# Scan of a hybrid prefix model on one Trainium2 core: output products with the two heads in turn, score products as two 64-row tiles

## The reference, cut to what matters

```
def step(s, inp):
    r_t, w_t, k_t, v_t, kk_t, a_t = inp
    sa = jnp.einsum("bhvk,bhk->bhv", s, kk_t)
    s = (s * w_t[:, :, None, :] - sa[..., None] * (kk_t * a_t)[:, :, None, :]
         + v_t[..., None] * k_t[:, :, None, :])
    return s, jnp.einsum("bhvk,bhk->bhv", s, r_t)
```

## Time and profile before

| | |
|---|---|
| Median of three runs | 2352.16 us (2350.6 to 2354.79) |
| Span of the profiled execution | 2351.2 us; the page gives no other time for it |
| Busy: PE | 1999.7 us (85%) |
| Busy: PE weight loads | 1426.2 us (61%) |
| Busy: DVE | 1150.0 us (49%) |
| Busy: ACT | 717.7 us (31%) |
| Busy: POOL | 179.3 us (8%) |
| DMA over the span | 291.82 MB, mean 124 GB/s |

### The profile page before, as it was taken

How to read it: one execution, slowest core, us unless ns; L and a number is a source line. 1 busy time by engine, 2 the same in 40 slices (tenths; PEclk the granted TensorE clock), 3 DMA queues, 4 the chain that set the end, 5 groups by cost and what they waited for, 6 DMA issues and landing times. The chain is left out here.

```text
span 2351.2 us, 28632 instructions
## 1 busy us (share of the span) xinstructions
PE 1999.7 (85%) x9873; PEld 1426.2 (61%) x9873; DVE 1150.0 (49%) x1761; ACT 717.7 (31%) x1046; POOL 179.3 (8%) x230
## 2 busy tenths in 40 slices
PE   5689988999998678889797989697868998899886
PEld 1356544555545447667684858484557777777774
DVE  0023321775000157373837456452167777777777
ACT  0312221110000231221313132220146666556564
POOL 0200003000001001010101010100100000000000
PEclk7789978999997689797878989695879999999998
DMA  9522131777220310000001000001157776777774
GB/s 381 188 87 68 53 119 68 235 252 249 55 106 18 107 32 19 15 18 7 25 0 32 0 15 0 2 1 73 54 180 254 251 269 237 281 278 266 256 255 160
DMA packets 148144, 291.82 MB, mean 124 GB/s; under 512 B 12115, under 2 KB 102277, under 8 KB 141829
## 3 DMA queue, kind: packets, MB, share of 16 engines
q1 hardware_dynamic: 125286, 198.25, 25.1%
q0 software_dynamic: 22816, 93.01, 11.2%
HBM read 288.45 MB, written 5.90 MB: 125 GB/s over the span
## 5 line engine op out<-in xcount | busy, mean ns | idle before, releaser
L2204 DVE TENSOR_TENSOR gate_up_low<-expert_gate_up,gate_up_high 128x1408 fp32r<-128x1408 f32 x146 | 234.9, 1624 | 73.5 <-ACT gate_up_high L2152 71.1
L2152 ACT ACTIVATE gate_up_high<-expert_gate_up 128x1408 fp32r<-128x1408 f32 x146 | 199.4, 1378 | 150.9 <-DMA expert_gate_up<-in_moe_w_up 80.5
L946 PE MATMUL banks<-normed_by_channel,gate_up_w 128*128 128x384 f32 x704 | 229.4, 489 | 7.1 <-DMA gate_up_w<-in_ffn_w_up 5.1
L2082 PE MATMUL banks<-gate_up_high,gathered_high 128*128 128x512 f32 (+1 forms) x432 | 171.4, 397 | 39.1 <-DVE gate_up_low L2204 38.8
L946 PEld LDWEIGHTS banks<-normed_by_channel,gate_up_w 128*128 128x128 f32 x704 | 134.3, 191 | 101.9 <-issue 8.1
L2084 PE MATMUL banks<-gate_up_high,gathered_low 128*128 128x512 f32 (+1 forms) x432 | 163.2, 378 | 0.0
L2083 PE MATMUL banks<-gate_up_low,gathered_high 128*128 128x512 f32 (+1 forms) x432 | 162.6, 376 | 0.0
L2200 DVE TENSOR_TENSOR down_low<-expert_down,down_high 128x1024 fp32r<-128x1024 f32 x99 | 118.8, 1223 | 30.1 <-ACT down_high L2146 26.1
L2082 PEld LDWEIGHTS banks<-gate_up_high,gathered_high 128*128 128x128 f32 x432 | 81.9, 190 | 66.6 <-DVE gate_up_low L2204 47.9
L2146 ACT ACTIVATE down_high<-expert_down 128x1024 fp32r<-128x1024 f32 x99 | 101.9, 1055 | 49.0 <-PE banks L2084 39.3
L955 PE MATMUL banks<-down_w,hidden 128*128 128x512 f32 x264 | 113.6, 592 | 1.4 <-DVE hidden L981 1.4
(11 more groups left out here) (385 smaller groups left out, 3437.1 us busy)
## 6 DMA issues: line engine op xcount, KB each, us to landing
expert_gate_up<-in_moe_w_gate SPq DMA_DIRECT2D x74, 704.0 KB, 5.9
expert_gate_up<-in_moe_w_up SPq DMA_DIRECT2D x74, 704.0 KB, 6.0
expert_down<-in_moe_w_down POOLq DMA_DIRECT2D x99, 512.0 KB, 6.0
mod_w_slots<-in_mod_w SPq DMA_DIRECT2D x24, 1024.0 KB, 22.9
next_mod_w<-in_mod_w POOLq DMA_DIRECT2D x24, 1024.0 KB, 5.4
gate_up_w<-in_ffn_w_gate SPq DMA_DIRECT2D x22, 512.0 KB, 4.1
gate_up_w<-in_ffn_w_up SPq DMA_DIRECT2D x22, 512.0 KB, 5.6
down_w<-in_ffn_w_down POOLq DMA_DIRECT2D x11, 1024.0 KB, 5.3
```

Source lines behind the costliest of these rows:

```text
L946: mm = nc.tensor.matmul(R.B[2 * p + m][:, 0:TOK], W[:, p, m, k, :], R.HT[:, k, :], start=(k == 0), stop=(k == KT - 1))
L2082: nc.tensor.matmul(out, a[0], b[0], start=first, stop=False)
L2152: nc.scalar.activation(WH[:, u % SPLIT, :], raw[:, u % RAW, :], ACT.Copy).then_inc(high, 1)
L2204: v.tensor_tensor(WL[:, u % SPLIT, :], raw[:, u % RAW, :], WH[:, u % SPLIT, :], ALU.subtract).then_inc(low, 1)
```

## The change

The left operands lose their zeros: `be` and `kt` become one array each for both heads, made by one VectorE instruction each. A score product takes the 64 partitions of its head alone, as weights and as moving operand; the order of heads and directions is swapped, so that the heads follow each other. The output products of a token tile are put in three groups by kind (Q2, then U, then the states), and within each group the heads follow each other. The number of products is the same; the four memsets before the loop go.

```diff
-        ka, rh, be, kt = E1, E2, sb("beta", [P, 2, 2, TOK]), sb("k_grown", [P, 2, 2, TOK])
+        ka, rh, be, kt = E1, E2, sb("beta", [P, 2, TOK]), sb("k_grown", [P, 2, TOK])
...
-                            for h in range(2):
-                                out = score_bank(t, i, h).rearrange("p (m d n) -> p m d n", m=2, d=2)
-                                for d in range(2):
-                                    mm = nc.tensor.matmul(out[:, :, d, :], left[:, h, d, cols], E12[:, :, d, cols], start=True, stop=True)
+                            for d in range(2):
+                                for h in range(2):
+                                    hr = slice(64 * h, 64 * h + 64)
+                                    out = score_bank(t, i, h).rearrange("p (m d n) -> p m d n", m=2, d=2)
+                                    mm = nc.tensor.matmul(out[:, :, d, :], left[hr, d, cols], E12[hr, :, d, cols], start=True, stop=True)
...
                     for t in range(TT):
-                        for h in range(2):
-                            hr = slice(64 * h, 64 * h + 64)
-                            for d in range(2):
-                                q = 2 * d + h
-                                out = B[4][hr, t * P:(t + 1) * P]
-                                nc.tensor.matmul(out, TM[:, t, 6, hr], Q2[:, t, q, :], start=(d == 0), stop=False)
-                                nc.tensor.matmul(out, U[:, t, d, h, :], Q1[:, t, q, :], start=False, stop=False)
-                                for cp in range(2):
-                                    ch = 2 * t + cp
+                        halves_of = [slice(64 * h, 64 * h + 64) for h in range(2)]
+                        for d in range(2):
+                            for h, hr in enumerate(halves_of):
+                                nc.tensor.matmul(B[4][hr, t * P:(t + 1) * P], TM[:, t, 6, hr], Q2[:, t, 2 * d + h, :], start=(d == 0), stop=False)
+                        for d in range(2):
+                            for h, hr in enumerate(halves_of):
+                                nc.tensor.matmul(B[4][hr, t * P:(t + 1) * P], U[:, t, d, h, :], Q1[:, t, 2 * d + h, :], start=False, stop=False)
+                        for d in range(2):
+                            for ch in (2 * t, 2 * t + 1):
+                                for h, hr in enumerate(halves_of):
                                     mm = nc.tensor.matmul(B[4][hr, ch * C:(ch + 1) * C], ST[hr, d, before_slot(d, ch), :],
-                                                          rh[hr, d, ch * C:(ch + 1) * C], start=False, stop=(d == 1 and cp == 1))
+                                                          rh[hr, d, ch * C:(ch + 1) * C], start=False, stop=(d == 1 and ch % 2 == 1))
...
-                for h in range(2):
-                    other = slice(64 - 64 * h, 128 - 64 * h)
-                    v.memset(be[other, h, :, :], 0.0)
-                    v.memset(kt[other, h, :, :], 0.0)
...
-                    for h in range(2):
-                        hr = slice(64 * h, 64 * h + 64)
-                        v.tensor_tensor(be[hr, h, :, :], nka[hr, :, :], E3[hr, :, :], ALU.mult)
+                    v.tensor_tensor(be[:, :, :], nka[:, :, :], E3[:, :, :], ALU.mult)
                     v.tensor_tensor(ka[:, :, :], E1[:, :, :], two(kk[:, :]), ALU.mult)
                     v.tensor_tensor(rh[:, :, :], E2[:, :, :], two(z[:, 0, :]), ALU.mult)
-                    for h in range(2):
-                        hr = slice(64 * h, 64 * h + 64)
-                        i = v.tensor_tensor(kt[hr, h, :, :], km[hr, :, :], E3[hr, :, :], ALU.mult)
-                    i.then_inc(dve_done, dve_inc("ops"))
+                    v.tensor_tensor(kt[:, :, :], km[:, :, :], E3[:, :, :], ALU.mult).then_inc(dve_done, dve_inc("ops"))
```

## The result

The changed kernel takes 2242.77 us (median of four runs, 2236.03 to 2245.76); the kernel before took 2352.2 beside it (four runs, 2350.6 to 2354.79). The ratio is 0.9531, with a 95% interval of 0.9514 to 0.9548: faster by 4.5 to 4.9%. The forecast was 2255 with a range of 2232 to 2284. The profiled execution has a span of 2243.6 us. From the first L1353 product to the last step of the sixth pair's normalisation (the scan, worked out from the trace) it takes 650.2 us, where the kernel before takes 759.4: 109.2 us less; what lies ahead of and behind the scan changes by under 2 us.

The account below looks back on a forecast made before the run. Bound: six head pairs in sequence, TensorE, VectorE and ScalarE handing stages on, TensorE alone in the outputs. Savings 6 x (1.85 + 1.71 + 0.45 + 11.15) = 90.9, less 2.6, plus 9: 97; 2352.2 - 97 = 2255 us, range 2232 to 2284.

Parts of the forecast that it names:

- Operands (beta to the end of k_grown): Operand stage: two 64x768 products become one 128x768 for beta and for k_grown; 1.85 us saved per pair.
- First score wait, 3.87 to 2.18: Score stage: VectorE gets the first product sooner because two row tiles run side by side; 1.71 us saved per pair.
- Second score wait: Score stage: VectorE's wait for the second product falls from 0.75 to 0.30 us; 0.45 per pair.
- Clock between transposes and first level: Stage from L1393 to L1413: the clock falls in the other three pairs too; 2.6 us lost.
- Outputs at the low clock, 20.0 to 8.9: Output products: heads side by side and fewer shape changes, 2.94 us per token tile; 11.15 us saved per pair.
- Clock in the outputs and the projection behind: Outputs and next projection: clock rises for the last third and the projection in half the pairs; 9 us gained.
- only the shape changes go: Rival, outputs: accumulation into one bank holds the other half back; 16.5 us per pair, 2310 us in all; chance 0.04.
- a turn empties the array: Rival, outputs and scores: each turn between heads costs 0.19 us like a change of shape; slower, 2387 us; chance 0.03.
- State products don't overlap: Rival, outputs: one bank keeps state products one after the other; 2.6 us per pair, 2270 to 2279 us; chance 0.15.
- that rival: Rival, scores: row tiles don't overlap with two directions in a strided output; 13 us lost, 2268 us; chance 0.05.
- high clock in all outputs: Rival, outputs: the clock is high in all output stages, with twice the work in flight; 2228 us; chance 0.10.

Follow-up runs that it names:

- outputs alone: The kernel before with only the new order of the output products, operands and score products as before: 2264.25 us, ratio 0.9623.
- grouped order: The changed kernel with, in each group of a tile, all output products of the first head before all of the second: 2268.36 us, ratio 0.9657.
- with one bank and with two: The changed kernel writes both heads' outputs to bank 4; a variant put the second head's in bank 5, with two ScalarE copies: 2247.8 us.
- fillers alone: The changed kernel plus unread TensorE products: eight per pair behind the last scores, 2241.51 us; with four more ahead of first scores, 2239.73 us.
- scores by head: The changed kernel with both directions of the first head before both of the second in the score products: 2244.99 us, ratio 0.9539.
- with the projection first: The changed kernel with half of the next pair's value projection ahead of the outputs instead of behind them: 2253.96 us, ratio 0.959.

## Why the prediction was right

The sum of the prediction's steps was 97 us; the scan lost 109.2. The measured 2242.8 lies inside the range but just under the spread that the forecast gave itself (2244 to 2268), and one term is why. By the trace, over six pairs:

| Step | Predicted, us | Measured, us |
|---|---|---|
| Operands (beta to the end of k_grown) | 11.1 | 11.0 |
| First score wait, 3.87 to 2.18 | 10.3 | 10.1 |
| Second score wait | 2.7 | 4.9 |
| Clock between transposes and first level | -2.6 | -4.3 |
| Outputs at the low clock, 20.0 to 8.9 | 66.9 | 66.7 |
| Clock in the outputs and the projection behind | 9 | 17.2 |
| Chain, and the stretch behind the outputs | 0 | 3.5 |

**Outputs.** The step held as it was put. A low-clock tile takes 2.96 us (predicted 2.94), the heads' passes start as neighbours, and the order alone accounts for 3.8 of the 4.7% (outputs alone). The rival "only the shape changes go" (16.5 us a stage) fell; the grouped order showed that even without turns TensorE overlaps part of the heads by itself. The rival "a turn empties the array" fell: passes of the two heads start 6 to 12 ns apart, where it needed 0.12 us per turn. The price of a change of shape, 0.19 us, came out at 0.2. "State products don't overlap" fell, with one bank and with two.

**Scores.** Row tiles overlap with a strided output as L1353 does with plain rows: 2.18 us where about 2.1 was expected, so that rival fell too. The second wait went wholly in the first pair, where 0.30 was expected: the clock rose while the second product ran (its eight passes from 890.91 to 892.49 take 1.58 us). In the sixth pair 0.29 is left.

**Operands.** The sum was right, its parts were not: beta itself falls from 3.48 to 0.96 us (its one instruction starts 0.05 us before GpSimd's first operation, as the first of its two did before and took 0.95; the second ran beside GpSimd and took 2.52), and `ka` and `rh` now run beside GpSimd's two operations and take 2.61 and 2.56 (2.46 and 0.95 before).

**The clock, the step that was mis-sized.** The prediction took a rise for the last third of the outputs in half of the pairs, 9 us. It came in all six, in the second tile already (after 5.4 to 5.8 us, 3.1 in the sixth pair), and the projection behind ran at 1.00 in all five pairs that have one: 9.2 + 8.0 = 17.2 us. That is 8.2 of the 12 us between sum and measurement; the second wait adds 2.2, the chain 2.0 (in the third and sixth pair of the kernel before it ran at 0.51) and the stretch behind the last outputs 1.6, and the transposes took 1.7 more than expected. The case "high clock in all outputs" (2228) lies 15 us under the result: the first 3 to 6 us of a stage still ran at 0.50.

That the clock is the doubtful term could have been read ahead: the earlier trace rows show the same stage at different clocks and different stages at constant ones. What no row of before could tell is how soon it would rise in the new order.

## What to carry to other kernels

Two products that each use half of the array took the time of one here, if they stand as neighbours in the program or within about four passes of each other: order small products by what part of the array they use, before thinking of fewer or larger ones, and group them by shape (0.15 to 0.2 us per change here). Where a stage runs at the low clock, look in the trace for what ran before the clock rose, give that term a wide range, and count a gain in clock as kept only when the period of the whole loop falls; here a filler that made one stage 1.14 us shorter lost it again in the stages behind. Then fill waits with work that has to be done anyway: that gained 11.5 us of the scan, where fillers alone gained 0.3 and 3.7.

## What the runs showed of the hardware that was not expected

- TensorE started passes ahead of passes that stand before them in the program, where they use another half of the array (grouped outputs, 955.16 between 955.15 and 955.37; scores by head, beside a pass four places ahead). The Trainium skill ("TensorE: Matmul & The Clock Gate", The mechanism) says that matmuls start and end strictly in order, without reordering. By the starts recorded here that doesn't hold between two halves of the array, and the times agree: a tile of the grouped outputs takes 4.33 us (954.25 to 958.59), where 16 + 16 passes one after the other would take 5.5 (an estimate from 0.213, 0.107 and 0.2 us per change of shape).
- In the kernel before, twenty microseconds of outputs without a gap, one head's part of the array at a time, ran at 0.50 from end to end in all six pairs, and the clock rose 2.4 to 4.7 us into the full-width projection behind them (from its length and mean clock). With the heads in turn it rose 5.4 to 5.8 us into the outputs, 3.1 in the sixth pair; with the projection first, 5.4 us into it in three pairs and 2.9 in two. So a TensorE without gaps did not bring the clock up by itself here. What does, and why the time until the rise differs, these runs don't settle.
- The scan's length repeats far better than the run's: 650.2, 650.2 and 650.2 us in three profiled executions (changed kernel twice, scores by head), while the place where the scan starts ranged from 862 to 875 us over all kernels. A change in the scan of a few microseconds is read from that stretch, and can't be read from the medians.
